# Down projection of the second token half moved between the convolution's in products, with weight panels split ahead and kept in DRAM

## The chip, the cores and the metric

The kernel runs on one core of a Trainium2 chip. The metric is device time in microseconds (us) of one execution, the median of three runs. The engines are TensorE (PE, with its weight loads PEld), VectorE (DVE), ScalarE (ACT), GpSimd (POOL) and SyncE (SP), which issues most transfers. Each works through its own list of instructions in order and waits for the others by semaphores.

## The reference

Two blocks follow one another on 1024 tokens of width 1024: a first block (attention, RWKV, merge, gated feed-forward) and a second (a convolution of 31 taps with its in and out projection, then an MLP of 4096). What the change touches:

```python
# end of the first block
h = rms_norm(x, norm_ffn_g)
gp = dwconv_centered(h @ w_ffn_gate, ffn_conv_w, ffn_conv_b)     # 3 taps
x = x + (silu(gp) * (h @ w_ffn_up)) @ w_ffn_down                 # 2816 hidden
# second block, conformer_conv on rms_norm_2(x)
a, g = split(x @ w_in + b_in, 2)                                 # 2 x 1024
h = a * sigmoid(g)
h = conv31_causal_depthwise(h, conv_w) + conv_b
h = silu(layer_norm(h, ln_g, ln_b))
x = x + h @ w_out + b_out
x = x + square(relu(rms_norm_2(x) @ w1)) @ w2
```

## The kernel before, in words

Activations lie transposed: 128 channels on the partitions, 8 tiles deep, tokens along the row. Tokens are worked in two halves of 512 (`h` 0 and 1); one matmul moves 512 tokens through 128x128 weights. Every product is done in three matmuls, high by high, high by low and low by high, of operands that are split into a rounded part (`hi`) and its remainder (`lo`).

Weights come as panels of 128x2048 (1 MB). SP loads one into one of three `raw` buffers (L276, `panel_sp`) as soon as the panel three before it is split; ACT rounds it into `whi` (L283), DVE subtracts into `wlo` (L287); both exist twice, and ACT waits until PE has done with the panel two before.

The feed-forward (`ffn_pe`, `ffn_dve`, `ffn_act`, `ffn_pool`) takes 22 hidden channels of 128, two to a block, 11 blocks. A channel is a gate and an up product, 48 matmuls each for both halves. DVE scales the gate (L2347), runs the 3 taps (L2352, L2356), ACT takes the SiLU (L2376), POOL multiplies by the norm (L2389), DVE by the up product (L2361), and ACT and DVE split the result into `aH` and `aL` (L2381, L2364). After block b's channels PE does the down product of block b - 1, 8 outputs n, and DVE adds each into `xT` (L2309).

Products land in 8 banks of PSUM, taken in turn (`ring`); PE waits for a bank until its last content is read.

Then the convolution's stage (`late_pe` and its fellows): for each of 8 channels the in products of both halves, gated to `u`; then 31 taps per channel and half. DVE does 26 of them (L2630), PE 5 by matmuls against diagonals that ACT makes (L2603, L2590); in the first half channels 6 and 7 have 12 and 20 on PE (`MORE`). The second half's DVE taps are spread over later work by `fill_dve`. Mean, variance, norm and SiLU of the first half come next (L2506, L2510, L2662, L2675, L2680), the out product `co_pe` (L2705 and L2441), and the MLP (`up_pe`, L2765 for its first product, and `back_pe`). All orders are written out by hand in `late_pe`, `late_dve`, `late_act`, `late_pool` and `late_sp`.

Of the kernel before, what the change touches and what calls it, by code (L numbers as in the profile page):

```python
# [213 lines left out]
def build(nc, A, out):  # L214
# [2120 lines left out]
    def ffn_dve(e):
# [4 lines left out]
        for blk in range(11):  # L2340
            for k in range(2):
# [916 lines left out]
```

## Time and profile before

| | us |
|---|---|
| median of the runs (3269.22 to 3271.22) | 3270.68 |
| profiled execution | 3276.46 |
| its span, first to last instruction | 3274.6 |
| PE busy in the span | 3152.3 (96%) |
| DVE busy | 2012.7 (61%) |
| ACT busy | 1067.3 (33%) |
| POOL busy | 374.1 (11%) |

Busy times and shares are of the profiled execution. Its feed-forward runs from about 1466 to 2175.91 us, the convolution's stage from there to 2516.7, the MLP (with the second half's out product in it) to the end. A PE that is shown busy has matmuls in its pipe; the mean clock granted to it was 0.982 of full speed. The chain of waits is followed back from the last instruction, at each step to what released it.

### The profile page before, as it was taken

How to read it: one execution, taken by the hardware profiler on the slowest of the kernel's cores; microseconds unless marked ns; L12 is line 12 of the kernel's file. 1: busy time of each engine (PE TensorE's matmuls, PEld its weight loads, DVE VectorE, ACT ScalarE, POOL GpSimd, SP SyncE). 2: the span in 40 equal slices, each digit the busy share in tenths (PEclk: the TensorE clock that was granted, in tenths of full speed). 3: DMA queues.
4: the chain of work that ended last, by engine and by line, in shares of the span. 5: the costliest groups of instructions: out<-in, count | busy, mean ns of one | idle time of the engine just before them, and what ended most of it. 6: DMA issues, size and time to landing. Idle time of an engine off the chain costs nothing.

```text
span 3274.6 us, 54823 instructions
## 1 busy us (share of the span) xinstructions
PE 3152.3 (96%) x23414; PEld 2544.0 (78%) x23414; DVE 2012.7 (61%) x3047; ACT 1067.3 (33%) x1528; POOL 374.1 (11%) x354
## 2 busy tenths in 40 slices
PE   8998998899999998999999999999999999999999
PEld 7787886777777777778888888887746888788887
DVE  6665554466766775545444444469979988755544
ACT  5222334445444443222111111132253333433332
POOL 0222441000000000301000000020000000110000
PEclk9999999799999999999999999999999999999999
DMA  3343665122222223421111111111101222223222
GB/s 148 126 135 99 214 213 186 54 75 81 69 86 75 82 81 116 148 90 52 39 52 52 52 42 49 52 39 52 39 13 52 103 91 103 90 90 126 94 91 76
DMA packets 93537, 288.80 MB, mean 88 GB/s; under 512 B 12400, under 2 KB 38640, under 8 KB 72816
## 3 DMA queue, kind: packets, MB, share of 16 engines
q1 hardware_dynamic: 79104, 233.39, 21.1%
q0 software_dynamic: 14192, 51.91, 4.6%
q8 instruction: 186, 3.05, 0.4%
q14 instruction: 55, 0.45, 0.0%
HBM read 228.64 MB, written 56.62 MB: 87 GB/s over the span
## 4 chain that ended last, share of the span: by engine, by line
PE 82%; DVE 10%; ACT 2%; issue 2%; DMA 2%; POOL 1%; SPq 1%; DVEq 0%; ACTq 0%; POOLq 0%
PE ps L2441 24%; PE ps L307 21%; PE ps L489 7%; PE ps L1744 4%; PE ps L2247 3%; PE ps L2603 2%; PE ps L1755 2%; DVE Yh L2630 2%; PE ps L1767 2%; PE ps L2063 1%; PE ps L1387 1%; PE ps L1404 1%; PE ps L1008 1%; PE ps L1398 1%; DVE wlo L287 1%
## 5 line engine op out<-in xcount | busy, mean ns | idle before, releaser
L2441 PE MATMUL ps<-Hh,whi 128*128 128x512 f32 x1600 | 497.6, 392 | 1.3 <-DVE uA L2562 0.7
L283 ACT ACTIVATE whi<-raw 128x2048 fp32r<-128x2048 f32 x139 | 265.5, 1910 | 522.2 <-PE ps L307 296.1
L287 DVE TENSOR_TENSOR wlo<-raw,whi 128x2048 fp32r<-128x2048 f32 x139 | 321.2, 2311 | 95.0 <-ACT whi L283 94.6
L2441 PEld LDWEIGHTS ps<-Hh,whi 128*128 128x128 f32 x1600 | 300.0, 188 | 70.5 <-issue 5.3
L2441 PE MATMUL ps<-Hh,wlo 128*128 128x512 f32 x800 | 311.4, 389 | 0.0
L307 PE MATMUL ps<-Hhi,wlo 128*128 128x512 f32 x672 | 206.9, 389 | 0.0
L307 PE MATMUL ps<-Hlo,whi 128*128 128x512 f32 x672 | 206.9, 389 | 0.0
L307 PE MATMUL ps<-Hhi,whi 128*128 128x512 f32 x672 | 206.8, 389 | 0.0
L2441 PE MATMUL ps<-aHh,whi 128*128 128x512 f32 x512 | 199.5, 390 | 2.7 <-DVE wlo L287 2.5
L2441 PE MATMUL ps<-aLh,whi 128*128 128x512 f32 x512 | 199.2, 389 | 0.0
L2441 PE MATMUL ps<-aHh,wlo 128*128 128x512 f32 x512 | 199.2, 389 | 0.0
L2809 DVE TENSOR_TENSOR xT<-ps,xT 128x512 f32<-128x512 f32 x256 | 169.2, 687 | 21.3 <-PE ps L2441 21.3
L2441 PEld LDWEIGHTS ps<-Hh,wlo 128*128 128x128 f32 x800 | 150.2, 188 | 31.5
L489 PE MATMUL ps<-Hhi,whi 128*128 128x512 f32 (+1 forms) x512 | 163.8, 401 | 0.0
L2309 DVE TENSOR_TENSOR xT<-ps,xT 128x512 f32<-128x512 f32 x176 | 112.3, 686 | 77.0 <-PE ps L307 76.0
L2630 DVE SCALAR_TENSOR_TENSOR Yh<-uB,vc,Yh 128x512 f32<-128x512 f32 x208 | 157.8, 761 | 3.0
L489 PE MATMUL ps<-Hlo,whi 128*128 128x512 f32 (+1 forms) x512 | 158.9, 392 | 0.0
L489 PE MATMUL ps<-Hhi,wlo 128*128 128x512 f32 (+1 forms) x512 | 158.0, 390 | 0.0
L2795 DVE TENSOR_TENSOR aLh<-rth,aHh 128x512 fp32r<-128x512 f32 x64 | 43.5, 722 | 170.2 <-ACT aHh L2789 170.2
L307 PEld LDWEIGHTS ps<-Hhi,wlo 128*128 128x128 f32 x672 | 126.1, 188 | 26.2
L307 PEld LDWEIGHTS ps<-Hhi,whi 128*128 128x128 f32 x672 | 126.1, 188 | 26.2
L307 PEld LDWEIGHTS ps<-Hlo,whi 128*128 128x128 f32 x672 | 126.1, 188 | 26.2
(389 smaller groups left out, 6181.8 us busy)
## 6 DMA issues: line engine op xcount, KB each, us to landing
raw<-in_panels SPq DMA_DIRECT2D x139, 1024.0 KB, 4.8
rwf<-F POOLq DMA_DIRECT2D x16, 1280.0 KB, 6.6
L<-rwf SPq DMA_DIRECT2D x16, 1024.0 KB, 5.0
L<-rwf SPq DMA_DIRECT2D x64, 256.0 KB, 3.5
gts<-so POOLq DMA_DIRECT2D x16, 512.0 KB, 3.5
gl<-gts SPq DMA_DIRECT2D x32, 256.0 KB, 3.6
rwt<-so POOLq DMA_DIRECT2D x15, 512.0 KB, 2.9
qkd<-XTs POOLq DMA_DIRECT2D x16, 384.0 KB, 4.0
```

Of the source, the lines that this page charges most:

```text
L283: e.activation(whi[i % 2][:, :], raw_of(i)[:, :], AF.Copy).then_inc(*a_hi.up(i))
L287: e.tensor_tensor(wlo[i % 2][:, :], raw_of(i)[:, :], whi[i % 2][:, :].bitcast(F32), OP.subtract).then_inc(*v_lo.up(i))
L307: m = e.matmul(aps[h][0:n1 - n0, :], w[wi][:, kc, n0:n1], mov[mi][:, kc, hs(h)], start=x == 0 and q == 0, stop=x == len(kcs) - 1 and q == 2)
L489: m = e.matmul(aps[h][0:n1 - n0, :], W[wi][:, kc, n0:n1], H2[mi][:, kc, hs(h)], start=kc == 0 and q == 0, stop=kc == 7 and q == 2)
L1744: m = e.matmul(bank[4 + half], Qb[g % 3][:, h, :], Kp[k % 2][:, h, hs(half)], start=True, stop=True)
L1755: m = e.matmul(bank[7][64 * n:64 * n + 64, 128 * (w % 4):128 * (w % 4) + 128], Vp[(w // 8) % 2][:, i, 64 * n:64 * n + 64], PT[:, i, n, :], ...
L1767: m = e.transpose(bank[6][:, 128 * q:128 * (q + 1)], Pb[w % 2][:, 128 * i:128 * (i + 1)], ident)
L2247: m = e.matmul(aps[h], W[wi][:, kc, n0:n0 + 128], H2[mi][:, kc, hs(h)], start=kc == 0 and q == 0, stop=kc == 7 and q == 2)
L2309: e.tensor_tensor(xT[:, n, hs(h)], ring.bank("down", p, n, h), xT[:, n, hs(h)], OP.add).then_inc(*v.up("x", b, n, h))
L2441: m = e.matmul(ap, W[wi][:, kc, n0:n0 + 128], mov[mi][:, kc, :], start=x == 0 and q == 0, stop=x == len(kcs) - 1 and q == 2)
L2630: e.scalar_tensor_tensor(out=to, in0=x, scalar=w, in1=to, op0=OP.mult, op1=OP.add).then_inc(*v_e.up(*key))
L2809: e.tensor_tensor(xT[:, n, hs(h)], ring.bank("x", h, b, n), xT[:, n, hs(h)], OP.add).then_inc(*v_e.up("x", h, b, n))
```

## The change

The down product of the feed-forward is done there for the first token half alone: 8 single banks instead of 8 pairs per block (`down_pe`, `down_dve`). The second half's hidden values are split too, into `aX` and `aY`, and POOL stores them in DRAM (`hid_pool`). After the first half's in products, three groups `rest_pe` of 8, 8 and 6 hidden tiles load them back (`hb`) and do the second half's down product; then come the second half's in products.

The weights of these products, 8 panels `ci` and 12 new ones `fe` (the down weights in another cut), are split during the feed-forward's channels 0 to 19, in 40 halves of 128x1024 (512 KB): POOL loads one into `sraw`, ACT rounds it into `shi`, DVE subtracts into `slo`, which is the place of `sraw`, and POOL stores both in DRAM. SP loads them later as high and low (`pre_sp`), in three buffers, where before a raw panel came and was split.

The first half's taps are all on DVE (`on_pe` is 0 there), in pairs of channels that alternate (`TAPS_A`, `ahead_dve`). The copy of 30 columns from the first half to the second moves from POOL to DVE (`edge_dve`). The second half's taps start later.

```diff
 def uses():
-    half = PANELS.index("co0")
...
+    aX, aY = sb("aX", 168, [128, 2, 512], F32R), sb("aY", 172, [128, 2, 512], F32R)
...
+    def save_load(e, s):
+        i, cols_ = part_s(s)
+        if s:
+            e.wait_ge(*d_ss.by("save", s - 1, "lo"))
+        e.dma_start(sraw[:, :], A["panels"][PIX[SAVED[i]]][:, cols_]).then_inc(*d_sl.up("save", s, "in"))
...
+    def save_act(e, s):
+        e.wait_ge(*d_sl.by("save", s, "in"))
+        e.activation(shi[:, :], sraw[:, :], AF.Copy).then_inc(*a_ff.up("save", s))
...
+    def save_dve(e, s):
+        e.wait_ge(*a_ff.by("save", s))
+        e.tensor_tensor(slo[:, :], sraw[:, :], shi[:, :].bitcast(F32), OP.subtract).then_inc(*v_ff.up("save", s))
...
+    def save_store(e, s):
+        i, cols_ = part_s(s)
+        e.wait_ge(*v_ff.by("save", s))
+        e.dma_start(sph[i][:, cols_], shi[:, :].bitcast(F32)).then_inc(*d_ss.up("save", s, "hi"))
+        e.dma_start(spl[i][:, cols_], slo[:, :].bitcast(F32)).then_inc(*d_ss.up("save", s, "lo"))
+
+    def hid_pool(e, b):
+        e.wait_ge(*v_ff.by("lo1", b, 1))
+        e.dma_start(hdh[:, 2 * b:2 * b + 2, :], aX[:, :, :].bitcast(F32)).then_inc(*d_hid.up("hid", b, "hi"))
+        e.dma_start(hdl[:, 2 * b:2 * b + 2, :], aY[:, :, :].bitcast(F32)).then_inc(*d_hid.up("hid", b, "lo"))
...
         panel_pe(e, p)
         W = weights(p, 2)
...
         for n in range(8):
...
+            ap, waits = ring.take(("down", b, n), (v_ff, "x", b, n))
+            for w in waits:
+                e.wait_ge(*w)
...
+            for kc in range(2):
+                for q, (wi, mi) in enumerate(THREE):
+                    m = e.matmul(ap, W[wi][:, kc, 128 * n:128 * n + 128], (aH, aL)[mi][b % 2][:, kc, :],
+                                 start=kc == 0 and q == 0, stop=kc == 1 and q == 2)
+            m.then_inc(*t_ff.up("x", b, n))
...
         for n in range(8):
...
-            for h in range(2):
-                e.wait_ge(*t.by("x", b, n, h))
-                e.tensor_tensor(xT[:, n, hs(h)], ring.bank("down", p, n, h), xT[:, n, hs(h)],
-                                OP.add).then_inc(*v.up("x", b, n, h))
+            e.wait_ge(*t_ff.by("x", b, n))
+            e.tensor_tensor(xT[:, n, hs(0)], ring.bank("down", b, n), xT[:, n, hs(0)], OP.add).then_inc(*v_ff.up("x", b, n))
...
+                if 2 * ch < PIECES_S:
+                    save_dve(e, 2 * ch)
                 e.wait_ge(*g_ff.by(ch))
...
-                e.tensor_tensor(aL[blk % 2][:, k, :], cv, aH[blk % 2][:, k, :].bitcast(F32),
+                e.tensor_tensor(aL[blk % 2][:, k, :], cv[:, hs(0)], aH[blk % 2][:, k, :].bitcast(F32),
                                 OP.subtract).then_inc(*v_ff.up("lo", blk, k))
+                e.wait_ge(*a_ff.by("hi1", ch))
+                e.tensor_tensor(aY[:, k, :], cv[:, hs(1)], aX[:, k, :].bitcast(F32),
+                                OP.subtract).then_inc(*v_ff.up("lo1", blk, k))
+                if 2 * ch + 1 < PIECES_S:
+                    save_dve(e, 2 * ch + 1)
             if blk:
...
+                if 2 * ch < PIECES_S:
+                    save_act(e, 2 * ch)
                 e.wait_ge(*v_ff.by("c2", ch))
                 e.activation(cv, cv, AF.Silu).then_inc(*a_ff.up("silu", ch))
...
+                if blk:
+                    e.wait_ge(*d_hid.by("hid", blk - 1, "lo"))
+                e.activation(aX[:, k, :], cv[:, hs(1)], AF.Copy).then_inc(*a_ff.up("hi1", ch))
+                if 2 * ch + 1 < PIECES_S:
+                    save_act(e, 2 * ch + 1)
...
+        save_load(e, 0)
         for ch in range(22):
             e.wait_ge(*a_ff.by("silu", ch))
             e.tensor_tensor(cv, cv, rs2, OP.mult).then_inc(*g_ff.up(ch))
+            if ch and ch % 2 == 0:
+                hid_pool(e, ch // 2 - 1)
+            for s in (2 * ch, 2 * ch + 1):
+                if s < PIECES_S:
+                    save_store(e, s)
+                if s + 1 < PIECES_S:
+                    save_load(e, s + 1)
+        hid_pool(e, 10)
...
-    MORE = {6: 12, 7: 20}
...
+    TAPS_A = [(2 * p + k, q) for p in range(4) for q in range(31) for k in range(2)]
...
+    def rest_pe(e, g):
+        for m_ in range(4):
+            W = pre_pe(e, 8 + 4 * g + m_)
+            if m_ == 0:
+                e.wait_ge(*d_hb.by("hb", g, "hi"))
+                e.wait_ge(*d_hb.by("hb", g, "lo"))
+            for k in range(2):
+                n = 2 * m_ + k
+                half_pe(e, ("x1", g, n), (v_e, "x1", g, n), W, 128 * k, hb[g], range((8, 8, 6)[g]))
+
+    def rest_dve(e, g, n):
+        e.wait_ge(*t_e.by("x1", g, n))
+        if g:
+            e.wait_ge(*v_e.by("x1", g - 1, n))
+        e.tensor_tensor(xT[:, n, hs(1)], ring.bank("x1", g, n), xT[:, n, hs(1)], OP.add).then_inc(*v_e.up("x1", g, n))
...
     def late_pe(e):
         first_pe(e, 0)
+        for ch in range(2, 8):
+            in_pe(e, 0, ch)
+        for g in range(3):
+            rest_pe(e, g)
         first_pe(e, 1)
-        taps_pe(e, 0, 0)
-        for ch in range(2, 8):
-            in_pe(e, ch)
-            taps_pe(e, 0, ch - 1)
-        taps_pe(e, 0, 7)
-        taps_pe(e, 1, 0)
+        for ch in range(2, 6):
+            in_pe(e, 1, ch)
         mean_pe(e, 0)
-        taps_pe(e, 1, 1)
-        taps_pe(e, 1, 2)
+        in_pe(e, 1, 6)
         var_pe(e, 0)
-        for ch in range(3, 6):
+        in_pe(e, 1, 7)
+        for ch in range(4):
             taps_pe(e, 1, ch)
         co_pe(e, 0)
-        taps_pe(e, 1, 6)
+        taps_pe(e, 1, 4)
         last_pe(e, 0)
-        taps_pe(e, 1, 7)
+        for ch in range(5, 8):
+            taps_pe(e, 1, ch)
...
     def late_dve(e):
-        done["B"] = 0
...
-        first_lo_dve(e, 1, range(4))
         recip_dve(e, ("sum2", 0), 0)
-        first_lo_dve(e, 1, range(4, 8))
-        e.wait_ge(*g_ff.by(21))
+        e.wait_ge(*v_e.by("rs", "sum2", 0))
+        in_dve(e, 0, 0)
+        in_dve(e, 0, 1)
+        for ch in range(2, 8):
+            ahead_dve(e, 10)
+            in_dve(e, 0, ch)
+        for g in range(3):
+            for n in range(8):
+                ahead_dve(e, 4 if g == 2 else 6)
+                rest_dve(e, g, n)
+                if g == 2 and n:
+                    first_lo_dve(e, 1, range(n - 1, n))
+        first_lo_dve(e, 1, range(7, 8))
         mean_dve(e, ("sum2", 1), 1, 1e-6)
         recip_dve(e, ("sum2", 1), 1)
         e.wait_ge(*v_e.by("rs", "sum2", 1))
-        in_dve(e, 0)
-        panels_after(panel_dve, e, UIX["ci0"])
-        in_dve(e, 1)
-        panels_after(panel_dve, e, UIX["ci1"])
-        taps_dve(e, 0, 0, 31)
-        for ch in range(2, 8):
-            in_dve(e, ch)
-            taps_dve(e, ch - 1, 0, 8)
-            panels_after(panel_dve, e, UIX[f"ci{ch}"])
-            taps_dve(e, ch - 1, 8, 31)
-        taps_dve(e, 7, 0, 31)
-        fill_dve(e, 3)
+        for ch in range(4):
+            ahead_dve(e, (0, 8, 10, 10)[ch])
+            edge_dve(e, ch)
+            in_dve(e, 1, ch)
+        ahead_dve(e, 10)
+        edge_dve(e, 4)
+        in_dve(e, 1, 4)
+        ahead_dve(e, len(TAPS_A))
+        edge_dve(e, 5)
+        in_dve(e, 1, 5)
+        panel_dve(e, CO)
         sub_dve(e, 0)
-        fill_dve(e, 6)
+        edge_dve(e, 6)
+        in_dve(e, 1, 6)
         mean_dve(e, ("var", 0), 0, 1e-6)
-        fill_dve(e, 2)
         recip_dve(e, ("var", 0), 0)
         norm_dve(e, 0)
+        panel_dve(e, CO + 1)
         for ch in range(8):
             silu_lo_dve(e, 0, ch)
-            fill_dve(e, 1)
-        fill_dve(e, 8)
+        edge_dve(e, 7)
+        in_dve(e, 1, 7)
```

Below is what stands in the engines' lists, without row numbers. `cv` is the channel in work, `rs_229` the norm, `raw`, `whi` and `wlo` the panel, `sph` and `spl` the split panels in DRAM, `hdh` and `hdl` the hidden values there. First POOL in the feed-forward before: 22 multiplies and nothing else, then the squares of the next norm.

```order
L2168 TENSOR_TENSOR mix_218<-mix_218,gl_220 128x512 [waits d_ga0,a_mx]
L2168 TENSOR_TENSOR mix_219<-mix_219,gl_220 128x512 [waits d_ga0,a_mx]
L2389 TENSOR_TENSOR cv<-cv,rs_229 128x1024 [waits a_ff,v_h]
L2389 TENSOR_TENSOR cv<-cv,rs_229 128x1024 [waits a_ff] x21
L2464 TENSOR_TENSOR sgt_252<-uB_244,uB_245 128x512 [waits a_e]
L2464 TENSOR_TENSOR sgt_252<-sgt_252,uB_244 128x512 [waits a_e,g_e]
```

POOL in the feed-forward now, from the first channel of a block to the start of the second:

```order
L2451 TENSOR_TENSOR cv<-cv,rs_229 128x1024 [waits a_ff]
L2334 DMA hdh<-aX 128x1024 [waits v_ff]
L2335 DMA hdl<-aY 128x1024
L2329 DMA sph<-shi 128x1024 [waits v_ff]
L2330 DMA spl<-slo 128x1024
L2316 DMA sraw<-in_panels 128x1024 [waits d_ss0]
L2329 DMA sph<-shi 128x1024 [waits v_ff]
L2330 DMA spl<-slo 128x1024
L2316 DMA sraw<-in_panels 128x1024 [waits d_ss0]
L2451 TENSOR_TENSOR cv<-cv,rs_229 128x1024 [waits a_ff]
```

Four stores and a load, two stores and a load now stand between two multiplies; each load waits for the stores ahead of it.

DVE at the end of a block before, from the second channel's gate (`gp`) to the adds of the down product (`xT`) and the next panel:

```order
L2347 TENSOR_TENSOR gp<-ps,rs_229 128x512 [waits t_ff]
L2352 TENSOR_SCALAR cv<-gp,vc 128x1024 [waits v_ff]
L2356 SCALAR_TENSOR_TENSOR cv<-gp,vc,cv 128x1024 [waits v_ff] x2
L2361 TENSOR_TENSOR cv<-ps,cv 128x512 [waits t_ff,g_ff]
L2361 TENSOR_TENSOR cv<-ps,cv 128x512 [waits t_ff]
L287 TENSOR_TENSOR wlo_57<-raw_52,whi_55 128x2048 [waits a_hi]
L2364 TENSOR_TENSOR aL_233<-cv,aH_231 128x1024 [waits a_ff]
L2309 TENSOR_TENSOR xT<-ps,xT 128x512 [waits t_ff] x16
L287 TENSOR_TENSOR wlo_56<-raw_53,whi_54 128x2048 [waits a_hi]
```

The same place now; `slo` is the subtraction for a half panel:

```order
L2393 TENSOR_TENSOR gp<-ps,rs_229 128x512 [waits t_ff]
L2398 TENSOR_SCALAR cv<-gp,vc 128x1024 [waits v_ff]
L2402 SCALAR_TENSOR_TENSOR cv<-gp,vc,cv 128x1024 [waits v_ff] x2
L2324 TENSOR_TENSOR slo<-sraw,shi 128x1024 [waits a_ff]
L2409 TENSOR_TENSOR cv<-ps,cv 128x512 [waits t_ff,g_ff]
L2409 TENSOR_TENSOR cv<-ps,cv 128x512 [waits t_ff]
L293 TENSOR_TENSOR wlo_56<-raw_52,whi_54 128x2048 [waits a_hi]
L2412 TENSOR_TENSOR aL_232<-cv,aH_230 128x512 [waits a_ff]
L2415 TENSOR_TENSOR aY<-cv,aX 128x512 [waits a_ff]
L2324 TENSOR_TENSOR slo<-sraw,shi 128x1024 [waits a_ff]
L2356 TENSOR_TENSOR xT<-ps,xT 128x512 [waits t_ff] x8
L293 TENSOR_TENSOR wlo_57<-raw_53,whi_55 128x2048 [waits a_hi]
```

Two subtractions have come in, one before the up product's multiply and one before the adds into `xT`; the adds are 8 instead of 16.

DVE at the first half's norm before, from the variance (`rsh_268`) to the low parts (`Hh_237`) with taps of the second half (`Yh_241`) between:

```order
L2506 TENSOR_SCALAR rsh_268<-ps 128x512 [waits t_e]
L2630 SCALAR_TENSOR_TENSOR Yh_241<-uB_244,vc,Yh_241 128x512 [waits v_e] x2
L2510 RECIPROCAL rsh_268<-rsh_268 128x512 [waits a_e]
L2675 TENSOR_TENSOR Yh_240<-Yh_240,rsh_268 128x512 [waits v_e]
L2675 TENSOR_TENSOR Yh_240<-Yh_240,rsh_268 128x512 x7
L2689 TENSOR_TENSOR Hh_237<-Yh_240,Hh_236 128x512 [waits a_e]
```

The same place now, with the last gated channel of the second half (`uT_262`) behind it:

```order
L2610 TENSOR_SCALAR rsh_283<-ps 128x512 [waits t_e]
L2614 RECIPROCAL rsh_283<-rsh_283 128x512 [waits a_e]
L2769 TENSOR_TENSOR Yh_247<-Yh_247,rsh_283 128x512 [waits v_e]
L2769 TENSOR_TENSOR Yh_247<-Yh_247,rsh_283 128x512 x7
L293 TENSOR_TENSOR wlo_56<-raw_53,whi_54 128x2048 [waits a_hi]
L2783 TENSOR_TENSOR Gh_246<-Yh_247,Gh_245 128x512 [waits a_e] x8
L2663 COPY uT_262<-uT_262 128x30 [waits v_e]
L2647 TENSOR_TENSOR sgt_268<-ps,rsh_284 128x512 [waits v_e,t_e]
L2651 TENSOR_TENSOR uT_262<-ps,rsh_284 128x512 [waits v_e,t_e]
L2654 SCALAR_TENSOR_TENSOR uT_262<-uT_262,vc,sgt_268 128x512 [waits v_e,a_e]
```

The second half's channel 7 is now gated after the first half's eight low parts; before, all gating was done ahead of the mean, and taps filled this place.

## Rows read from the trace of the kernel before

**Rows 1.** The page, busy us and share per engine.

```profile
PE 3152.3 (96%) x23414; PEld 2544.0 (78%) x23414; DVE 2012.7 (61%) x3047; ACT 1067.3 (33%) x1528; POOL 374.1 (11%) x354
```

**Rows 2.** Stretches: us, busy PE, PEld, DVE, ACT, POOL, clock, DMA share, GB/s.

```profile
1534.00:2096.00 562.00, 562.00 (x2481) 465.33 (x2481) 271.31 (x306) 83.96 (x60) 40.67 (x17) 1.00 0.14 48
2216.00:2379.00 163.00, 162.45 (x662) 124.34 (x663) 150.37 (x213) 37.32 (x63) 4.66 (x7) 1.00 0.13 46
```

**Rows 3.** The chain of waits in order: start us, us, what.

```profile
1479.59 696.32 PE ps L307 x3072
...
2390.10 17.42 PE ps L2603 x40
```

**Rows 4.** PE's waits from 2176 us on: total us, times, longest.

```profile
PE ps L2765 <- DVE Hh L2750: 4.2, 1, 4.2
PE ps L2441 <- DVE wlo L287: 3.1, 2, 2.5
PE ps L2480 <- ACT tl L2728: 2.3, 2, 1.3
```

**Rows 5.** The line of the taps on PE: ns min/median/max, starts.

```profile
L2603 PE MATMUL ps<-uA,dg x124: 590/592/667, 2222.1 to 2406.9; 128*128 128x512 f32 x124
```

**Rows 6.** DVE timeline, taps: start us, us; two alternating, three in succession.

```profile
2244.46 0.75 DVE L2630 SCALAR_TENSOR_TENSOR tl<-uA,vc,tl 128x512 f32<-128x512 f32 x1
2245.12 0.75 DVE L2630 SCALAR_TENSOR_TENSOR Yh<-uA,vc,Yh 128x512 f32<-128x512 f32 x1
...
2414.37 2.32 DVE L2630 SCALAR_TENSOR_TENSOR Yh<-uB,vc,Yh 128x512 f32<-128x512 f32 x3
```

**Rows 7.** Timelines of DVE and ACT at the first half's norm.

```profile
2440.95 3.35 DVE L2510 RECIPROCAL rsh<-rsh 128x512 f32<-128x512 f32 x1 [2.69 <-ACT rsh L2496]
2444.33 4.91 DVE L2675 TENSOR_TENSOR Yh<-Yh,rsh 128x512 f32<-128x512 f32 x8
...
2449.75 0.80 ACT L2680 ACTIVATE Yh<-Yh,vc 128x512 f32<-128x512 f32 x1
...
2451.12 0.80 ACT L2680 ACTIVATE Yh<-Yh,vc 128x512 f32<-128x512 f32 x1
```

**Rows 8.** DVE timeline of one feed-forward channel.

```profile
1838.51 1.29 DVE L2347 TENSOR_TENSOR gp<-ps,rs 128x512 f32<-128x512 f32 x2 [6.42 <-PE ps L307]
...
1851.56 2.29 DVE L287 TENSOR_TENSOR wlo<-raw,whi 128x2048 fp32r<-128x2048 f32 x1 [0.53 <-ACT whi L283]
1853.77 1.22 DVE L2364 TENSOR_TENSOR aL<-cv,aH 128x1024 fp32r<-128x1024 f32 x1
```

**Rows 9.** ACT and POOL timelines of the same channel.

```profile
1843.33 1.06 ACT L2376 ACTIVATE cv<-cv 128x1024 f32<-128x1024 f32 x1 [13.56 <-DVE cv L2356]
1851.43 1.04 ACT L2381 ACTIVATE aH<-cv 128x1024 fp32r<-128x1024 f32 x1
...
1844.46 2.39 POOL L2389 TENSOR_TENSOR cv<-cv,rs 128x1024 f32<-128x1024 f32 x1 [41.13 <-ACT cv L2376]
```

**Rows 10.** Transfers issued in 1534:2096, at 335.2, at 1382: KB, us to landing.

```profile
raw<-in_panels SPq DMA_DIRECT2D x26, 1024.0 KB, 4.8
...
gts<-so POOLq DMA_DIRECT2D x1, 512.0 KB, 3.0
...
xs<-in_xT SPq DMA_DIRECT2D x1, 512.0 KB, 3.6
```

**Rows 11.** The same, issued from 387.5 to 389.2 us.

```profile
raw<-in_panels SPq DMA_DIRECT2D x1, 1024.0 KB, 6.6
gts<-so POOLq DMA_DIRECT2D x1, 512.0 KB, 6.9
```

**Rows 12.** Stretches as in rows 2, around PE's wait before 2516.7 us.

```profile
2503.00:2508.00 5.00, 2.71 (x6) 0.79 (x5) 4.72 (x7) 2.26 (x3) 0.00 (x0) 1.00 0.04 15
...
2516.00:2522.00 6.00, 5.29 (x13) 4.21 (x14) 5.58 (x9) 2.57 (x5) 0.00 (x0) 0.50 0.00 0
2522.00:2525.00 3.00, 3.00 (x14) 2.46 (x13) 2.79 (x5) 1.34 (x3) 0.00 (x0) 0.91 0.00 0
```

More of the change, by code:

```diff
@@ L279, in panel_act @@
         e.wait_ge(*d_raw.by(i))
-        if i >= 2:
+        if i in (CO, CO + 1):
+            e.wait_ge(*t_e.by("gate", 1, 5 + i - CO))
+        elif i >= 2:
             sig, key = last_use.get(i - 2, (a_hi, (i - 2,)))
@@ L2406, in build @@
     tl_ = [sb(f"tl{i}", 200 + 2 * i, [128, 512])[:, :] for i in range(2)]
-    tq = [[uB[6 * h + i][:, 0:512] for i in range(2)] for h in range(2)]
+    tq = [[uT[8 + i][:, 0:512] for i in range(2)] for h in range(2)]
     aHh = [sb(f"aHh{i}", 152 + 8 * i, [128, 2, 512], F32R) for i in range(2)]
@@ L2518, in first_pe @@
             e.wait_ge(*w)
-        outs = outs_pe(e, [((x, h, 0), (v_e, x, h, 0), weights(p, 8), n0) for x, n0 in (("a", 0), ("gate", 128))])
+        outs = outs_pe(e, [((x, h, 0), (v_e, x, h, 0), W, n0) for x, n0 in (("a", 0), ("gate", 128))])
         for kc in range(8):
@@ L2550, in in_dve @@
-    def in_dve(e, ch):
-        for h in range(2):
-            u = u_of(h, ch)[:, 30:542]
-            e.wait_ge(*t_e.by("gate", h, ch))
-            if ch:
-                e.wait_ge(*v_e.by("u", h, ch - 1))
-            e.tensor_tensor(sgt[h], ring.bank("gate", h, ch), rsh[h], OP.mult).then_inc(*v_e.up("gate", h, ch))
-            e.wait_ge(*t_e.by("a", h, ch))
-            if h == 0 and ch >= 2:
-                e.wait_ge(*last_tap(0, ch - 2))
-                e.wait_ge(*v_e.by("taps", 0, ch - 2))
-                e.wait_ge(*g_e.by("tail", ch - 2))
-            e.tensor_tensor(u, ring.bank("a", h, ch), rsh[h], OP.mult).then_inc(*v_e.up("a", h, ch))
-        for h in range(2):
-            u = u_of(h, ch)[:, 30:542]
-            e.wait_ge(*a_e.by("sg", h, ch))
-            e.wait_ge(*v_e.by("a", h, ch))
-            e.scalar_tensor_tensor(out=u, in0=u, scalar=vec("a_b_in", ch), in1=sgt[h], op0=OP.add,
-                                   op1=OP.mult).then_inc(*v_e.up("u", h, ch))
@@ L2570, in in_act, with u_of, in_pe @@
-    def in_act(e, ch):
-        for h in range(2):
-            e.wait_ge(*v_e.by("gate", h, ch))
-            e.activation(sgt[h], sgt[h], AF.Sigmoid, bias=vec("a_b_in", 8 + ch)).then_inc(*a_e.up("sg", h, ch))
-    def tail_pool(e, ch):
-        e.wait_ge(*v_e.by("u", 0, ch))
-        e.tensor_copy(uB[ch][:, 0:30], uA[ch % 2][:, 512:542]).then_inc(*g_e.up("tail", ch))
+        in_pe(e, h, 1)
+    def u_of(h, ch):
+        return uB[ch] if h else uA[ch]
+    def in_pe(e, h, ch):
+        W = pre_pe(e, 20 * h + ch)
+        for x, n0 in (("a", 0), ("gate", 128)):
+            half_pe(e, (x, h, ch), (v_e, x, h, ch), W, n0, Hh[h], range(8))
@@ new lines, in in_dve @@
+    def in_dve(e, h, ch):
+        u = u_of(h, ch)[:, 30:542]
+        e.wait_ge(*t_e.by("gate", h, ch))
+        if ch >= 2:
+            e.wait_ge(*v_e.by("u", h, ch - 2))
+        e.tensor_tensor(sgt[ch % 2], ring.bank("gate", h, ch), rsh[h], OP.mult).then_inc(*v_e.up("gate", h, ch))
+        e.wait_ge(*t_e.by("a", h, ch))
+        if h:
+            e.wait_ge(*v_e.by("tail", ch))
+        e.tensor_tensor(u, ring.bank("a", h, ch), rsh[h], OP.mult).then_inc(*v_e.up("a", h, ch))
+        e.wait_ge(*a_e.by("sg", h, ch))
+        e.wait_ge(*v_e.by("a", h, ch))
+        e.scalar_tensor_tensor(out=u, in0=u, scalar=vec("a_b_in", ch), in1=sgt[ch % 2], op0=OP.add,
+                               op1=OP.mult).then_inc(*v_e.up("u", h, ch))
@@ L3034, in late_sp @@
     def late_sp(e):
-        panels_sp(e, UIX["mg0"] + 7, UIX["mu4'"])
+        panels_sp(e, UIX["mg0"] + 7, CO)
+        for j in range(3):
+            pre_sp(e, j)
+        hb_sp(e, 0)
+        for j in range(3, 28):
+            pre_sp(e, j)
+            if j in (10, 14):
+                hb_sp(e, j // 4 - 1)
+            if j == 24:
+                panel_sp(e, CO)
+        panels_sp(e, CO + 1, UIX["mu4'"])
         for n in range(8):
@@ L3218, in lay_out @@
         pan(f"fd{b}", fd[256 * b:256 * (b + 1)])
+    for g in range(3):
+        for m in range(4):
+            pan(f"fe{4 * g + m}", fd[1024 * g:min(1024 * (g + 1), 2816), 256 * m:256 * (m + 1)])
     ai, ao = np.asarray(a_w_in_2)[0], np.asarray(a_w_out_2)[0]
```

224 lines of the change are left out of this document (125 added, 99 removed).

## The prediction

> **What bounds the kernel now.** I read the page's first part, then the stage table, then the chain of waits, then one channel of the feed-forward on every engine, and last the transfers and the clock. TensorE is busy 96% of the span [rows 1]. In the feed-forward, 1534 to 2096 us, it has no gap: 562.00 of 562.00 us, with DVE at 271.31 and ACT at 83.96 [rows 2]. The chain shows it as one piece of 696.32 us with 3072 matmuls, 0.2267 us each, ending at 2175.91 [rows 3]. So there only the number of matmuls counts, and nothing on the other engines, while they keep up. In the convolution (2216 to 2444) TensorE is still nearly full, DVE nearly so too (150.37 of 163.00) [rows 2]. After the feed-forward PE waits little for others, the most at one place 4.2 us [rows 4].
>
> **What leaves TensorE.** Before, 62 taps of the first token half were matmuls against diagonals: 124 instructions [rows 5], two per tap. The chain has 20 taps (40 instructions) in 17.42 us, 0.87 each [rows 3]; the longest instructions, up to 667 ns against a median of 592 [rows 5], are few, so I take 0.86. All 62 go: 62 x 0.86 = 53.3 us less PE work. They go to DVE, where they hide: two channels now alternate, and alternating taps start 0.66 us apart, successive taps of one channel 0.77 [rows 6].
>
> **What only moves.** 22 x 8 x 3 = 528 down matmuls of the second half leave the feed-forward (-119.7 us) and come back between the in products (+119.7). The in products are the same 768 in another order. While these run, DVE has 10 taps and one gated channel per 48 matmuls: 10 x 0.66 + about 2.1 = 8.8 against 10.9 us; then 6 taps and an add, 4.6 against 5.4; then 4 taps, an add and a low part, 3.9 against 4.1. The loads there, two of 1 MB per product, take 3.0 + 3 x 1.8 = 8.4 us by the prices below, against 10.9 and three buffers deep. I cost them at nothing.
>
> The new order has waits of its own. The last 22 taps of the first half end about 1 us after PE asks for the mean. The second half's last gated channel stands on DVE behind mean, root and the first norm (I take 0.7 for each, a norm is 0.61), the reciprocal (3.35) and the eight low parts, which follow ACT at 1.37 us each [rows 7], 11.0 together; its own low part, gate, sigmoid and first diagonal add some 3.5. That is about 20 us from the variance sum, in which PE has one product of 10.9; the taps it has to go on with need that channel, so it waits about 9 us. Around the second group of taps I find 3 us more, and the clock falls once. Against that, the 4.2 us wait before the MLP goes (three channels of taps now lie there), with its own fall of the clock, and the late panel casts of the out projection mostly go. I set new against old waits at 0, bounds -8 and +12. The second half's taps start 13 later (14 issued before the out projection instead of 27) and end in MLP block 12 instead of 11: +1, bounds 0 and 13 x 0.77 = 10. Without the feed-forward the sum is -53.3 + 1 = -52.3.
>
> **What the feed-forward gets.** PE has 48 matmuls less per block, but 20 panels are now split there, in 40 halves of 512 KB, two per channel through channel 19. One half is a chain through one buffer: POOL issues the load, ACT casts, DVE subtracts into the loaded tile, POOL issues two stores, and the next load waits for the second to land. These steps stand in program order with work that is needed: the channel's SiLU stands on ACT behind a cast, the multiply of POOL behind a load, and the eight adds that empty the banks of the down projection stand on DVE behind the block's fourth subtraction. With 16 bank uses a block and 8 banks, the next block's first product takes the banks of the first two adds. So PE can start it only when the fourth half of the block is split.
>
> I count from G, the end of a block's first gate product (1838.5 in the channel shown). The POOL multiply ends at G + 8.35 [rows 8, 9]. Prices: a 512 KB POOL store lands 3.0 us after its issue, a 1 MB load 4.8, so each further 512 KB is taken as 1.8; a 512 KB load lands in 3.6 when SP issues it [rows 10]. No POOL load is in the trace: between 3.0 and 3.6 I take 3.3. A 128x1024 cast is 1.04, SiLU 1.06, a 128x1024 subtraction 1.22, two adds 1.29 [rows 8, 9].
>
> G + 8.35; the block's saved hidden values and the first half, four stores, 3.0 + 3 x 1.8 = 8.4: 16.75. Load 3.3, cast, subtraction: 22.3. Two stores 4.8, load 3.3, cast: 31.45. SiLU and multiply of the second channel (1.06, 2.39): 34.9. Two stores, load, cast, subtraction: 45.3. Two adds: 46.55, and 0.5 for some eight hand-overs: 47.0.
>
> PE is ready for the next block after 192 matmuls, G + 43.5. That is 3.5 us late without any collision. The panel loads on SP's queue collide with two of the three loads: each is issued when DVE has written wlo, at G + 15.1 and at 3.5 us after the second multiply, while the POOL loads are issued at G + 16.75 and 4.8 after it. A 512 KB store that was issued 0.7 us behind such a panel load took 6.9 instead of 3.0, the panel 6.6 instead of 4.8 [rows 11]. Even sharing until the smaller is through would cost the small one another 1.8. Bounds per collision 1.8 and 3.9; I take 1.8, which a share explains and which the panel itself lost. Wait per block 3.5 + 3.6 = 7.1 us, in blocks 1 to 9: 64 us.
>
> The Trainium skill (DMA: Bandwidth & Descriptors, section Queues, rings and completion order) says that the DMA engines alternate between queues at packet granularity. By that rule a collision costs a share, as I priced it; the row with 6.9 us speaks for more, and by it the total would be 3354.
>
> An idle PE also costs clock. After the idle 4.2 us before 2516.7 the granted clock was 0.50 (1.2 GHz) from 2516 to 2522 and 0.91 to 2525 [rows 12]; half speed lost 3.0 + 0.3 = 3.3 us. Waits of 1.3 us [rows 4] left it at 1.00 (2503 to 2508) [rows 12]. A wait of 7 us should cost this each time: 9 x 3.3 = 30. Block 0 has no down product to cover its fourth half: its chain runs some 5 us into block 1. Feed-forward: 64 + 30 + 5 = +99.
>
> **The sum.** -53.3 + 1 + 99 = +46.7 us. The profiled execution took 3276.46 us, a span of 3274.6 and 1.9 around it, so 3323 for a run like it; it lies 5.8 above the median of the runs. On the median, 3270.7 + 46.7 = 3317.
>
> **The rivals.**
> A, faster: the transfers overlap and the chain fits. If four stores land 4.8 after the first issue (three issues of 0.6, then 3.0), two in 3.6, and a load in 3.0, and SP's loads don't disturb, the chain is 47.0 - 3.6 - 2.4 - 0.9 = 40.1, below the 43.5 from which it decides; PE never waits, and -52.3 gives 3218. For it: stores landed in 3.0 in a busy stretch. Against it: 3 MB more in a channel of 27 us, and [rows 11].
> The Trainium skill (the same page, section with the two cost components) gives 2.0 us plus the bytes over 436 GB/s. An estimate by it alone prices 512 KB at 1.2 more, the chain at about 44.3 and the total at 3250 to 3275; the trace's 3.0 agrees, its 1.8 does not.
> B, a middle case: the chain is late by about 2.5 us, too little for the clock to fall: 9 x 2.5 = 23, so 3241. Only the price of 512 KB, between 0.6 and 1.8, decides between this and the forecast.
> C, slower elsewhere: the alternating taps run at 0.77, or a weight load comes late, and the convolution waits. 60 taps after the last deferred product x 0.11 = 6.6 us on top of the forecast: 3324. Against it: 0.66 [rows 6].
> Upper end: collisions at 3.9 each, a wait of 11.3 + 3.3 per block: 136 - 52 = +84, 3354.
>
> **How the numbers follow.** Forecast 0.66 (its own range 3285 to 3350), A 0.18, B 0.10, C 0.06. Changes within 0.2%, 6.5 us, are about what can't be told from none here. A and most of B are faster: 0.26; between the cases 0.05; slower 0.69. The range reaches from between A and B, 3238, to 3350.
>
> **What will show it.** Right: in the feed-forward PE waits once per block, for the first xT adds of the down projection, which stood on DVE behind the subtraction into slo; the granted clock falls after it; POOL's wait for stores fills its time; blocks 1 to 9 are about 65 us apart, block 10 is not. The stretch from the last down matmul of the feed-forward to the MLP's first matmul grows by 66 us (119.7 - 53.3), and no taps of the first half are left on PE. Wrong: PE without gaps between 1480 and the end of a feed-forward of 600 us (then A), or a convolution stage that grew by over 80 us.

## The result and the profile after

The changed kernel takes 3326.97 us (median of four runs, 3325.68 to 3328.86) against 3269.95 before: 1.0176 times as long, 95% interval 1.0158 to 1.0194, or 57 us more. The forecast was 3317, the range 3238 to 3350.

The profiled execution took 3326.56 us, its span 3324.8. Cut at the same four matmuls in both kernels (the first with the feed-forward's input, the first in product, the first of the MLP, the end), it reads:

| stage, us | before | after | difference | forecast |
|---|---|---|---|---|
| before the feed-forward (same code) | 1454.2 | 1449.5 | -4.7 | 0 |
| feed-forward | 721.6 | 705.0 | -16.6 | -20.7 (99 - 119.7) |
| convolution and first out product | 340.9 | 411.1 | +70.2 | +66.4 |
| MLP, second out product | 757.9 | 759.2 | +1.3 | +1 |

119.7 us of down products left the feed-forward; it became only 16.6 shorter. So it lost 103.1 us. The page's first line:

```profile
PE 3117.2 (94%) x23290; PEld 2533.6 (76%) x23290; DVE 2041.2 (61%) x3105; ACT 1075.0 (32%) x1515; POOL 448.7 (13%) x488
```

Against [rows 1] PE has 124 matmuls less, the taps, and is busy less of a longer span. Stretches of the new feed-forward and of the deferred down products, with the columns of [rows 2]:

```profile
1574.00:1960.00 386.00, 341.19 (x1443) 279.65 (x1444) 185.08 (x202) 84.39 (x78) 74.77 (x98) 0.93 0.44 165
...
2156.00:2447.00 291.00, 290.78 (x1264) 236.87 (x1263) 240.49 (x357) 32.06 (x43) 14.49 (x10) 1.00 0.60 235
```

In the first PE had no gap before [rows 2]; now 45 us in 386 are missing, at a mean clock of 0.93. In the second, deferred down products beside the first half's taps, PE is full, though the transfer engines are busy 60%. Three alternating taps of that stretch on DVE took 2.07 us of 0.75 each, so they start 0.66 apart:

```profile
2201.29 2.07 DVE L2727 SCALAR_TENSOR_TENSOR Yh<-uT,vc,Yh 128x512 f32<-128x512 f32 x3
```

PE's waits in the feed-forward (total us, times, longest):

```profile
PE ps L313 <- DVE xT L2356: 67.4, 9, 8.7
PE ps L2348 <- DVE cv L2409: 7.7, 1, 7.7
PE ps L2348 <- DVE gp L2393: 3.4, 1, 3.4
```

Nine times, ahead of blocks 2 to 10, PE stands before the next block's first gate product until DVE has added into `xT`. The chain of waits through one such block, from POOL's multiply of the first channel to that product (start us, us, what; pieces named "issue" between them left out):

```profile
1658.93 2.39 POOL cv L2451
...
1662.91 5.37 DMA spl<-slo
...
1668.57 5.45 DMA sraw<-in_panels
...
1674.04 1.07 ACT shi L2320
...
1675.13 1.24 DVE slo L2324
...
1677.18 3.78 DMA spl<-slo
...
1681.24 4.13 DMA sraw<-in_panels
...
1686.36 1.05 ACT cv L2431
...
1687.49 2.50 POOL cv L2451
...
1690.52 3.76 DMA spl<-slo
...
1694.56 5.36 DMA sraw<-in_panels
...
1699.94 1.06 ACT shi L2320
...
1701.03 1.23 DVE slo L2324
1702.25 1.21 DVE xT L2356 x2
...
1703.60 1.19 PE ps L313 x2
```

Read it from the end: the product waits for two adds, the adds for the subtraction of a half panel, that for the cast, that for a load, and the load for a store's landing. Nothing in it is PE's own work. From the end of the first multiply (1661.32) to the end of the two adds (1703.46) it is 42.1 us; the prediction's steps give 46.55 + 0.5 + 3.6 - 8.35 = 42.3. (G + 8.35 was its end of the multiply.)

The convolution's new wait, on DVE, ACT and PE (timelines: start us, us; x is how many):

```profile
2470.93 0.69 DVE L2783 TENSOR_TENSOR Gh<-Yh,Gh 128x512 fp32r<-128x512 f32 x1 [0.50 <-ACT Gh L2779]
...
2471.63 0.68 DVE L2647 TENSOR_TENSOR sgt<-ps,rsh 128x512 f32<-128x512 f32 x1
...
2473.10 0.75 DVE L2654 SCALAR_TENSOR_TENSOR uT<-uT,vc,sgt 128x512 f32<-128x512 f32 x1 [0.19 <-ACT sgt L2659]
```

```profile
2473.89 4.49 ACT L2692 ACTIVATE dg<-cc,vc 128x128 f32<-128x128 f32 x15 [0.82 <-DVE uT L2654]
```

```profile
2474.43 15.74 PE L2705 MATMUL ps<-uT,dg 128*128 128x512 f32 x30 [9.34 <-ACT dg L2692]
```

The last gating stands behind the eighth low part (`Gh`), and PE waits 9.34 us for the first diagonal; about 9 were forecast. The 4.2 us of [rows 4] before the MLP are gone.

### The profile page after: what moved, and what is told of

It is laid out like the page before. It is cut to its first block, busy times and chain, and to the rows that moved or that the text cites. A ratio compares the mean times of both kernels' runs of the same rounds, so it can differ in the third digit from the quotient of the medians.

```text
span 3324.8 us, 54774 instructions
## 1 busy us (share of the span) xinstructions
PE 3117.2 (94%) x23290; PEld 2533.6 (76%) x23290; DVE 2041.2 (61%) x3105; ACT 1075.0 (32%) x1515; POOL 448.7 (13%) x488
## 4 chain that ended last, share of the span: by engine, by line
PE 68%; DVE 11%; DMA 9%; ACT 4%; POOL 3%; issue 3%; SPq 0%; DVEq 0%; ACTq 0%; POOLq 0%
PE ps L2545 27%; PE ps L495 7%; PE ps L313 5%; DMA sraw<-in_panels 4%; DMA spl<-slo 4%; PE ps L1750 3%; PE ps L2253 2%; PE ps L1761 2%; PE ps L1773 1%; PE ps L2069 1%; POOL cv L2451 1%; PE ps L1393 1%; PE ps L1410 1%; PE ps L2705 1%; PE ps L1014 1%
## 5 line engine op out<-in xcount | busy, mean ns | idle before, releaser
L293 DVE TENSOR_TENSOR wlo<-raw,whi 128x2048 fp32r<-128x2048 f32 x131 | 301.6, 2302 | 75.8 <-ACT whi L289 75.6
L289 ACT ACTIVATE whi<-raw 128x2048 fp32r<-128x2048 f32 x131 | 250.0, 1908 | 294.9 <-PE ps L2545 201.8
L2727 DVE SCALAR_TENSOR_TENSOR Yh<-uT,vc,Yh 128x512 f32<-128x512 f32 x448 | 326.7, 767 | 11.8 <-ACT Yh L2712 8.6
L2545 PE MATMUL ps<-Hh,whi 128*128 128x512 f32 x1024 | 317.1, 391 | 0.6 <-DVE wlo L293 0.6
L313 PE MATMUL ps<-Hhi,whi 128*128 128x512 f32 x672 | 215.8, 403 | 67.4 <-DVE xT L2356 67.4
L2545 PEld LDWEIGHTS ps<-Hh,whi 128*128 128x128 f32 x1024 | 192.2, 188 | 42.6 <-issue 1.9
L2545 PE MATMUL ps<-Hh,wlo 128*128 128x512 f32 x512 | 199.2, 389 | 0.0
L2903 DVE TENSOR_TENSOR xT<-ps,xT 128x512 f32<-128x512 f32 x256 | 169.2, 685 | 20.2 <-PE ps L2545 20.2
L2545 PE MATMUL ps<-Gh,whi 128*128 128x512 f32 x576 | 181.2, 396 | 0.0
L2324 DVE TENSOR_TENSOR slo<-sraw,shi 128x1024 fp32r<-128x1024 f32 x40 | 49.0, 1224 | 184.6 <-ACT shi L2320 184.6
L2320 ACT ACTIVATE shi<-sraw 128x1024 fp32r<-128x1024 f32 x40 | 42.4, 1060 | 358.3 <-DMA sraw<-in_panels 358.3
```

The lines of the kernel that those rows point to most:

```text
L289: e.activation(whi[i % 2][:, :], raw_of(i)[:, :], AF.Copy).then_inc(*a_hi.up(i))
L293: e.tensor_tensor(wlo[i % 2][:, :], raw_of(i)[:, :], whi[i % 2][:, :].bitcast(F32), OP.subtract).then_inc(*v_lo.up(i))
L313: m = e.matmul(aps[h][0:n1 - n0, :], w[wi][:, kc, n0:n1], mov[mi][:, kc, hs(h)], start=x == 0 and q == 0, stop=x == len(kcs) - 1 and q == 2)
L2320: e.activation(shi[:, :], sraw[:, :], AF.Copy).then_inc(*a_ff.up("save", s))
L2324: e.tensor_tensor(slo[:, :], sraw[:, :], shi[:, :].bitcast(F32), OP.subtract).then_inc(*v_ff.up("save", s))
L2545: m = e.matmul(ap, W[wi][:, kc, n0:n0 + 128], mov[mi][:, kc, :], start=x == 0 and q == 0, stop=x == len(kcs) - 1 and q == 2)
```

## The experiments

Theory: one buffer for loading, splitting and storing makes a serial chain per half panel, and the adds into `xT` stand behind the fourth link. Rivals: the traffic itself, or DVE's load. All kernels were timed beside the kernel before; each table entry is the median, with the ratio to it and its 95% interval.

| kernel | us | ratio | feed-forward | convolution stage |
|---|---|---|---|---|
| changed kernel | 3326.97 | 1.0176 (1.0158 to 1.0194) | 705.0 | 411.1 |
| e1_adds_first | 3243.53 | 0.9922 (0.9903 to 0.9940) | 624.6 | 412.1 |
| e2_own_place | 3232.73 | 0.9888 (0.9873 to 0.9903) | 612.9 | 411.1 |
| e4_one_store | 3249.65 | 0.9943 (0.9924 to 0.9961) | 628.1 | 412.1 |
| e3_taps_alone | 3284.40 | 1.0051 (1.0034 to 1.0068) | 721.3 | 357.1 |
| e5_gate_early | 3228.16 | 0.9870 (0.9854 to 0.9887) | 609.3 | 408.8 |
| e6_all_three | 3218.18 | 0.9841 (0.9824 to 0.9858) | 605.2 | 407.5 |

**The order on DVE.**

```diff
-    def down_dve(e, b):
+    def down_dve(e, b, s):
         for n in range(8):
...
+        if s < PIECES_S:
+            save_dve(e, s)
...
-                if 2 * ch + 1 < PIECES_S:
+                if 2 * ch + 1 < PIECES_S and k == 0:
                     save_dve(e, 2 * ch + 1)
             if blk:
-                down_dve(e, blk - 1)
-        down_dve(e, 10)
+                down_dve(e, blk - 1, 2 * ch + 1)
+            elif blk == 0:
+                save_dve(e, 2 * ch + 1)
+        down_dve(e, 10, PIECES_S)
```

> The changed kernel with one order turned round on DVE: the fourth subtraction of a block stands behind the eight adds into xT, not ahead of them. Theory (the adds are late only because they stand behind the fourth half panel): the nine waits for xT, 67.4 us, and the clock lost behind them, about 1.8 us each, go. The chain of the saves itself, from POOL's multiply of one block to that of the next, adds up to about 54.0 us by the changed kernel's trace, just under PE's 54.4, so little wait is left: 3327 - 84 = 3243, up to 3255. Rival 1, the chain needs more than a block's time and PE waits elsewhere, for the gate or the up product, by 2 to 3 us a block: about 3268. Rival 2, the cause is not this order but the traffic or DVE's load: 3327.

Measured 3243.53. Same bytes, same instructions, one subtraction per block later in DVE's list, and 83 us are gone. PE's waits in the same stretch of this kernel:

```profile
PE ps L2348 <- DVE cv L2411: 8.7, 1, 8.7
PE ps L313 <- DVE xT L2356: 4.1, 4, 2.1
```

67.4 us for `xT` became 4.1. Neither traffic nor DVE's load, both unchanged, is the cause. The wait of 8.7 in block 1, for the up product's multiply, remains.

**A place for slo.**

```diff
-    rs2 = sb("rs2", 198, [128, S])[:, :]
+    rs2 = sb("rs2", 196, [128, S])[:, :]
...
-    sraw, slo, shi = sb("sraw", 176, [128, 1024]), sb("slo", 176, [128, 1024], F32R), sb("shi", 180, [128, 1024], F32R)
+    sraw, slo, shi = sb("sraw", 176, [128, 1024]), sb("slo", 200, [128, 1024], F32R), sb("shi", 180, [128, 1024], F32R)
...
         if s:
-            e.wait_ge(*d_ss.by("save", s - 1, "lo"))
+            e.wait_ge(*v_ff.by("save", s - 1))
         e.dma_start(sraw[:, :], A["panels"][PIX[SAVED[i]]][:, cols_]).then_inc(*d_sl.up("save", s, "in"))
...
         e.wait_ge(*d_sl.by("save", s, "in"))
+        if s:
+            e.wait_ge(*d_ss.by("save", s - 1, "lo"))
         e.activation(shi[:, :], sraw[:, :], AF.Copy).then_inc(*a_ff.up("save", s))
```

> The changed kernel with a place of its own for slo (rs2 moves to make room), so that the next half's load waits for the subtraction and not for the stores; the next cast waits for them. Same bytes, same order. Theory (serial landings through one buffer): a load runs beside the stores, the chain from a block's gate product to the fourth subtraction falls from 51 to about 40 us, below the 43.5 that PE needs; all of the 103 us that the feed-forward gained goes, or all but 5: 3224 to 3232. Rival (the bytes, not the waits, take the time; loads beside stores take twice as long): half of it goes, about 3265 to 3275.

Measured 3232.73, 0.7 past the slow end of the theory's range; 92 of the 103.1 us of the feed-forward are back. Its chain of waits from 1640 to 1780 us is PE alone:

```profile
1665.25 43.52 PE ps L313 x192
1708.77 10.88 PE ps L2350 x48
1719.65 43.52 PE ps L313 x192
```

A block takes 54.40 us. The loads did get slower beside the stores, and PE did not wait for it here. The tile `sraw` in this kernel and in the changed one (us to landing, min, median, max):

```profile
DMA to landing us min/median/max: 4.6/5.4/8.6
```

```profile
DMA to landing us min/median/max: 3.3/5.2/6.9
```

One wait of 7.2 us for `xT` is left, early on. So either edit alone, the order or the place, takes most of the loss away: the late adds need both the serial chain and their place behind its fourth link.

**The price of a store.**

```diff
     def save_store(e, s):
...
         e.dma_start(sph[i][:, cols_], shi[:, :].bitcast(F32)).then_inc(*d_ss.up("save", s, "hi"))
-        e.dma_start(spl[i][:, cols_], slo[:, :].bitcast(F32)).then_inc(*d_ss.up("save", s, "lo"))
```

The kernel leaves out the low parts of the saved panels and computes with the high parts in their place.

> The changed kernel without the store of the low parts of the saved panels; later the high parts are loaded in their place, so that the later loads are the same in number and size. It prices a second 512 KB store. Three such stores stand in the chain ahead of the first late add. At the prediction's 1.8 us each the wait per block falls from 7.5 to 2.1 and the clock stays up: 9 x (5.4 + 1.8) = 65 less, 3262. At 1.5 each: 9 x 4.5 = 40 and part of the clock, about 3275 to 3287. If bytes beside bytes cost next to nothing (0.7 or less): 3305 or more.

Measured 3249.65, below all three expected times. The chain of waits through one block, up to a wait of PE of 1.56 us:

```profile
1798.79 2.38 POOL cv L2450
...
1802.24 5.12 DMA sph<-shi
...
1807.64 4.73 DMA sraw<-in_panels
...
1815.01 2.89 DMA sph<-shi
...
1818.19 3.32 DMA sraw<-in_panels
...
1835.45 1.23 DVE slo L2324
1836.67 1.21 DVE xT L2355 x2
```

From the end of the multiply (1801.17) to the end of the adds (1837.88) it is 36.7 us, 5.4 less than with three more stores. That is 3 x 1.8, but 1.8 is not the price of a store. A pair of stores from the end of the subtraction to the next load's issue took 1681.24 - 1676.37 = 4.87, one store 1818.19 - (1813.49 + 1.24) = 3.46, so 1.4. At the other two places it was 7.25 against 6.47 (four stores against three) and 4.58 against 3.24, so 0.8 and 1.3. In these two blocks, one of either kernel, the three stores cost 3.5 us together, 1.2 each. The other 1.9 came from loads that were faster (4.73 against 5.45, 3.32 against 4.13, 5.04 against 5.36). The total fell 12 us further than 1.8 per store gives: PE's waits in blocks 0 and 1 shrank too, and in four of the nine places there was none at all.

**The taps without the deferral.**

```diff
     def on_pe(h, ch):
-        return MORE.get(ch, NPE) if h == 0 else NPE
+        return NPE if h else 0
```

The waits and the lists of PE and ACT that named these taps are changed to match.

> The kernel before, with the first token half's 62 taps on DVE instead of PE and nothing else moved (the down products stay in the feed-forward). PE has 53 us less work. DVE gets 62 x 0.66 = 41 us more in a stretch of 228 us in which it was 92% busy. Theory (DVE can take the taps only because the deferred down products stretch the stage): the stage becomes bound by DVE, 210 + 41 = 251 instead of 228 us, the total about 3290 (3280 to 3300). Rival (DVE's taps hide beside PE's work as they are): 3270 - 53 = 3217.

Measured 3284.40, 15 us slower than before (expected about 20). PE's waits in its convolution stage, and its stretch from 2216 to 2444 us:

```profile
PE ps L2480 <- DVE Yh L2639: 30.4, 2, 19.2
PE ps L2602 <- ACT dg L2589: 26.1, 2, 25.7
```

```profile
2216.00:2444.00 228.00, 164.09 (x620) 118.82 (x620) 217.58 (x320) 34.96 (x55) 4.00 (x6) 0.87 0.09 33
```

DVE is busy 217.58 of 228 and PE waits for its taps. PE loses the same 124 instructions as in the changed kernel, but only beside the deferred down products do DVE's taps hide. The expectation had taken DVE's 92% from the shorter stretch to 2379 us of [rows 2]; over the 228 us the kernel before shows 193.65, 85%:

```profile
2216.00:2444.00 228.00, 224.73 (x804) 150.51 (x805) 193.65 (x271) 70.19 (x138) 5.33 (x8) 1.00 0.11 37
```

With that its sum would have been 194 + 41 = 235 and not 251, 7 us more than before. The stage grew by 16.2, so the total came near the forecast in part by luck. That DVE's taps set the time is shown by the waits; the price of it was not well forecast.

**The late gating.**

```diff
+        edge_dve(e, 7)
-        for ch in range(8):
+        for ch in range(3):
             silu_lo_dve(e, 0, ch)
-        edge_dve(e, 7)
         in_dve(e, 1, 7)
+        for ch in range(3, 8):
+            silu_lo_dve(e, 0, ch)
```

On ACT likewise: the sigmoid and 15 diagonals after three of the eight.

> slo in its own place as in e2_own_place, and in the convolution's stage the second half's channel 7 is gated, and its first 15 diagonals are made, after three of the first half's eight low parts, no longer behind all eight. Theory (PE's 9.3 us wait for the first diagonal comes from what stands ahead of it on DVE and ACT, not from the gate product): the product ends, gate 0.7, a switch of ACT's table 1.3 and the sigmoid 0.7, the product with the gate 0.7, first diagonal 0.3, so the wait falls to about 3.8 us; the four channels of taps cover the rest of the low parts. 5.5 us and some clock less than e2_own_place's 3233: 3225 to 3228. Rival (the low parts then come late and the out projection waits for them, or the two more table loads cost it): 3233 or more.

Measured 3228.16, 4.6 us less than e2_own_place; by stages 2.3 less in the convolution. The wait fell from 9.3 to 5.7, not to 3.8:

```profile
PE ps L2707 <- ACT dg L2694: 9.3, 3, 5.7
```

I had left out what stands ahead of the three low parts in any case: the eight norms and a panel's low part (2.29 us). The shorter wait is shown. That the kernel as a whole is faster is not: the two intervals overlap, the two profiled executions took 3228.87 and 3228.81 us, and the feed-forward, which this edit leaves alone, was 3.6 us shorter as well.

**All three.** The two edits above and e1_adds_first's in one kernel.

> e5_gate_early and the adds into xT ahead of the fourth subtraction, as in e1_adds_first. In e2_own_place one wait for xT is left, 7.2 us after block 0, where no down product covers the fourth half panel. Theory: only block 0's subtraction, which has no adds ahead of it in either order, stands behind that wait, so the turned order doesn't shorten it and the time is e5_gate_early's, within 3 us. Rival (the order also relieves block 1): 8 us less, about 3218. If adds and the next panel's subtraction get in each other's way: 3 to 6 us more.

Measured 3218.18, the lowest median: 0.9841 of the kernel before. My expectation fell, since the wait that was left got shorter. The chain of e5_gate_early into it:

```profile
1552.98 1.06 ACT shi L2322
1554.06 1.22 DVE slo L2326
1555.29 1.21 DVE xT L2358 x2
```

These are block 0's adds, done in block 1, behind block 1's fourth subtraction; I had taken the wait for one at block 0's own end. With the adds first it is 2.2 us instead of 6.4. So the rival's mechanism, that the order also relieves block 1, is shown, but its 8 us are not. The two profiled executions lie 12.1 us apart: 4.1 of it in the feed-forward, 1.3 in the convolution and 6.7 before the feed-forward, the last two in code that is the same. That the total met the rival's 3218 is in part luck. The feed-forward is now 605.2 us, 3.3 above the 601.9 that are left of the 721.6 before when the moved 119.7 are taken off.

## Why the prediction was right, step by step

- **The taps, -53.3, and the moved products, 0.** The stage grew by 70.2, of which 66.4 was forecast as work. Waits, taken as 0 net (bounds -8 and +12), came to +2.8: 13.1 us after, 12.9 of them for diagonals and 9.3 at one place, against 10.3 before, of which the 4.2 of [rows 4] is one. The granted clock was 0.50 behind the 9.3 us wait until about 2479.7, which costs some 2.6. The remaining -1.6 has no place in this account.
- **The MLP, +1.** Measured +1.3, but not as priced. The last tap of the second half starts at 2840.58 on DVE, POOL's sum behind it holds PE 4.0 us, and the clock is at 0.50 for some 5.5 us after it (2.7 lost). Against that, the slow clock after the 4.2 us wait (2.9 lost) is gone, and waits for panels fell from 3.1 to 1.9. These four add up to +2.6, 1.3 more than was measured.
- **The place of the wait.** Right to the instruction: next block's first product, two adds, the fourth subtraction.
- **The chain.** 42.3 forecast, 42.1 measured, but two errors cancel. The stores took 7.25 + 4.87 + 4.58 = 16.7 us where 8.4 + 4.8 + 4.8 = 18.0 was forecast, and the three loads 5.45 + 4.13 + 5.36 = 14.9 instead of 3 x 3.3 + 3.6 = 13.5. The 1.8 per further 512 KB set a 1 MB load (4.8) against a 512 KB store (3.0); the two loads of [rows 10] differ by 4.8 - 3.6 = 1.2, and 1.2 is what e4_one_store measured per store. The estimate under rival A took the same 1.2. So close an agreement in the sum is luck; the serial chain itself is what e1_adds_first and e2_own_place show.
- **The collisions, 1.8 each.** In the whole feed-forward the 12 loads into `sraw` with no panel load beside them took 3.3 to 4.2 us, the 19 that were issued up to 1.2 us behind one took 5.1 to 6.9. In the block shown the two took 1.2 to 1.3 more than the 4.13 of the third. The Trainium skill (DMA: Bandwidth & Descriptors, section Queues, rings and completion order) has the engines alternate between queues by packets; the trace agrees that a collision costs a share, and doesn't show the alternation itself.
- **Waits, 64 us.** 67.4, nine times 7.5 instead of 7.1.
- **Block 0, 5 us.** Mis-sized: 7.7 + 3.4 = 11.1, both in block 1. In blocks 0 and 1 the chain had fallen so far behind that the up product's multiply and the gate's scaling, which stand behind subtractions too, came late for the down product. I followed the chain to the adds alone.
- **The clock, 30 us.** Mis-sized: 3.3 per wait was carried over from one row group. The eight pitches from 1574.70 to 2087.77 are 513.1 us; less 8 x 54.4 of work and 59.0 of waits 18.9 are left, 2.4 each. What of the 103.1 is no wait is 24.6. Waits 3.4 over, block 0 6.1 over and the clock 5.4 under make the feed-forward's 4.1; here too errors cancel.
- **The sum.** The medians differ by 57.0, the forecast was 46.7. The stages that the change touches grew by 54.9, so 8.2 of the 10.3 us missing lie in the terms above (feed-forward 4.1, convolution 3.8, MLP 0.3). The other 2.1 is scatter: the profiled executions differ by 50.1 and not by 57.0, with 4.7 of their difference before the feed-forward.
- **The rivals.** **A** needed stores and loads that overlap; four stores took 7.25 us, not 4.8. e2_own_place, where a load may run beside the stores, took 3232.73 against A's 3218, so such a time is within reach, but only with a second place. **B** was to hold if a further 512 KB cost less than 1.8. It cost 1.2, and the waits were still 7.5 us, since loads took more than was forecast. B also took a wait of 2.5 us as too short for the clock to fall; the last section shows that some of this length lowered it. **C** had no part: the deferred products run with PE full, and taps start 0.66 us apart.

## What to carry to other kernels

A transfer through one buffer (load, cast, subtract in place, store, load again) runs at the sum of its latencies, however little any engine is busy; give the result its own place before asking how many bytes it moves. In an in-order engine, work that nobody waits for soon belongs behind work that frees a buffer, not ahead of it: here the position of one subtraction per block was worth 83 us. When work is taken off the full engine, price what the other engines' programs now put in front of it.

## What the runs showed of the hardware

The clock falls while PE idles, so a long wait pays part of the slow time while it does nothing. Stretches around one wait of 8.7 us in the changed kernel, then around the 4.2 us of the kernel before (columns as in [rows 2]; the sixth number behind the comma is the granted clock):

```profile
1630.00:1632.00 2.00, 1.19 (x6) 0.65 (x4) 1.04 (x2) 0.00 (x0) 0.54 (x1) 1.00 0.50 100
1632.00:1634.00 2.00, 0.00 (x0) 0.00 (x0) 0.00 (x0) 0.00 (x0) 0.00 (x0) 0.80 1.00 410
1634.00:1636.00 2.00, 0.00 (x0) 0.00 (x0) 0.00 (x0) 0.00 (x0) 0.00 (x0) 0.50 0.76 299
...
1640.00:1642.00 2.00, 2.00 (x5) 1.61 (x6) 2.00 (x4) 0.00 (x0) 0.00 (x0) 0.50 0.93 369
1642.00:1644.00 2.00, 2.00 (x7) 1.52 (x7) 2.00 (x4) 0.00 (x0) 0.50 (x1) 0.64 0.35 141
```

```profile
2514.00:2516.00 2.00, 0.00 (x0) 0.00 (x0) 1.93 (x4) 0.76 (x2) 0.00 (x0) 0.93 0.64 270
```

After 8.7 us of idling PE worked at 0.50 (1.2 GHz) for some 3.5 us, until about 1643.4; after 4.2 us, in which it had only just fallen, it did so for some 5.8, from 2516.7 to about 2522.5 [rows 12]. In e4_one_store the waits of 2.6, 0.3 and 1.6 us left the clock at 1.00. The one of 2.8 us, which ended at 1895.46, did not, though the first two matmuls behind it took 0.70 us together as behind the others:

```profile
1895.50:1897.50 2.00, 2.00 (x8) 1.61 (x9) 2.00 (x4) 0.00 (x0) 0.00 (x0) 0.80 0.69 270
1897.50:1900.00 2.50, 2.50 (x7) 1.96 (x6) 2.50 (x4) 0.00 (x0) 0.54 (x1) 0.50 0.40 121
```

The length of a short wait doesn't settle it. PE waits 2.65 us at the start of the feed-forward in every kernel here: in six of them the first two matmuls then took 1.19 us together, in e5_gate_early and e6_all_three 0.70, and the products of this first part took 25.1 us in the changed kernel and 23.8 in those two. That is part of the 3.6 us by which e5_gate_early's feed-forward is shorter than e2_own_place's. Judge the clock by the granted clock of the 5 us behind a wait, not by its first matmuls.

The part before the feed-forward is the same code in all kernels of this study save for where its results lie, and its length in the profiled executions went from 1442.0 to 1454.2 us. A difference of up to some 12 us between two profiled executions is better read from the stage than from the total.
